# A hybrid pooling and attention layer: the gates by tanh in place of exponential, addition, reciprocal and product

## The reference, cut to what matters

```python
hn = _rmsnorm(h, norm_g[layer])
proj = hn @ w_in[layer]
pv, pg, q, k, v, ag = jnp.split(proj, SPLITS, axis=-1)
pool_out = _multiscale_pool(pv, pool_w[layer], pool_scale[layer])
attn_out = _attention_branch(q, k, v, q_norm_g[layer], k_norm_g[layer], sinks[layer])
mixed = jnp.concatenate([jax.nn.silu(pg) * pool_out,
                         jax.nn.silu(ag) * attn_out], axis=-1)
h = h + mixed @ w_out[layer]
```

## Time and profile before

| what | value |
|---|---|
| three runs | 1301.02, 1302.70 and 1302.71 us, median 1302.7 us |
| span of the profiled execution | 1300.8 us |
| the profiled execution's own time | not given apart from its span |
| TensorE busy (matmul) | 1279.3 us, 98% of the span |
| VectorE busy | 895.0 us, 69% |
| ScalarE busy | 634.8 us, 49% |
| TensorE clock granted | full (1.000 on average) |
| HBM traffic | 103 GB/s on average |

### The profile page before, as it was taken

One profiled execution on the slowest core, in us unless ns is written; L12 is line 12 of the kernel. 1 busy time (PEld: TensorE's weight loads), 2 busy tenths in 40 slices (PEclk: granted clock), 3 DMA queues, 4 the chain that ended last, 5 costly groups with the idle time before them and its releaser, 6 DMA issues.

```text
span 1300.8 us, 19299 instructions
## 1 busy us (share of the span) xinstructions
PE 1279.3 (98%) x6200; PEld 1057.4 (81%) x6200; DVE 895.0 (69%) x1417; ACT 634.8 (49%) x1490; POOL 66.5 (5%) x78
## 2 busy tenths in 40 slices
PE   4999999999999999999999999999999999999998
PEld 4988798798888987888888887787887877788887
DVE  7466777878868777665644677777787887854553
ACT  6434356365454554545433344554645545444442
POOL 0000000010010110000000000000101103000000
PEclk9999999999999999999999999999999999999999
DMA  5233322322322225544543332223222222244442
GB/s 213 79 92 97 90 72 75 89 68 63 94 81 75 67 73 185 188 133 157 186 127 89 92 98 86 70 73 88 83 72 79 84 81 74 93 141 137 161 140 86
DMA packets 70609, 134.38 MB, mean 103 GB/s; under 512 B 8064, under 2 KB 10240, under 8 KB 69888
## 3 DMA queue, kind: packets, MB, share of 16 engines
q1 hardware_dynamic: 68160, 125.17, 31.4%
q0 software_dynamic: 2384, 8.39, 1.8%
HBM read 125.14 MB, written 8.39 MB: 103 GB/s over the span
## 4 chain that ended last, share of the span: by engine, by line
PE 94%; DVE 3%; DMA 1%; ACT 1%; issue 1%; SPq 0%; ACTq 0%
PE R L1058 18%; PE R L1059 18%; PE R L1062 18%; PE S L1281 4%; PE S L1282 4%; PE S L1280 4%; PE S L1181 3%; PE S L1180 3%; PE OP L1282 2%; PE OP L1280 2%; PE R L1281 2%; PE OP L1281 2%; PE R L1282 2%; PE R L1280 2%; PE OP L1059 1%; PE OP L1062 1%
## 5 line engine op out<-in xcount | busy, mean ns | idle before, releaser
L430 ACT ACTIVATE wh<-raw 128x512 fp32r<-128x512 f32 x400 | 250.3, 631 | 534.7 <-PE R L1062 310.1
L725 DVE TENSOR_TENSOR wl<-raw,wh 128x512 fp32r<-128x512 f32 x400 | 281.7, 708 | 264.7 <-ACT wh L430 263.6
L1058 PE MATMUL R<-act_h,wh 128*128 128x512 f32 (+1 forms) x1168 | 426.0, 370 | 0.0
L1059 PE MATMUL R<-act_l,wh 128*128 128x512 f32 (+1 forms) x1168 | 422.8, 367 | 0.0
L1062 PE MATMUL R<-act_h,wl 128*128 128x512 f32 (+1 forms) x1168 | 403.5, 366 | 0.0
L1058 PEld LDWEIGHTS R<-act_h,wh 128*128 128x128 f32 x1168 | 220.1, 188 | 36.4 <-DVE wl L725 0.8
L1059 PEld LDWEIGHTS R<-act_l,wh 128*128 128x128 f32 x1168 | 220.1, 188 | 34.7
L1062 PEld LDWEIGHTS R<-act_h,wl 128*128 128x128 f32 x1168 | 210.6, 188 | 36.7
L948 DVE RECIPROCAL scr<-scr 128x512 f32<-128x512 f32 x32 | 107.3, 3353 | 1.1
L402 POOL TENSOR_TENSOR scr<-scr 128x527 f32<-128x527 f32 (+3 forms) x40 | 48.7, 1217 | 837.6 <-ACT pv_last L430 378.2
L430 ACT ACTIVATE pm<-OP 16x128 fp32r<-16x128 f32 x256 | 68.1, 266 | 5.4
(11 more groups left out here) (210 smaller groups left out, 1844.5 us busy)
## 6 DMA issues: line engine op xcount, KB each, us to landing
raw<-w_in_blocks SPq DMA_DIRECT2D x272, 256.0 KB, 2.6
raw<-w_out_in SPq DMA_DIRECT2D x128, 256.0 KB, 3.0
scr<-xcat SPq DMA_DIRECT2D x32, 256.0 KB, 4.4
mixed<-xcat SPq DMA_DIRECT2D x4, 1024.0 KB, 7.7
res<-xcat SPq DMA_DIRECT2D x16, 256.0 KB, 3.2
out<-scr POOLq DMA_DIRECT2D x14, 256.0 KB, 2.6
out<-res POOLq DMA_DIRECT2D x14, 256.0 KB, 4.2
scr<-pool_w_in SPq DMA_DIRECT2D x8, 256.0 KB, 3.0
```

The costliest lines, as they stand in the source:

```text
L430: return nc.scalar.activation(dst, src, ACT.Copy)
L725: return nc.vector.tensor_tensor(dst, a, b, ALU.subtract)
L1058: mm(o, wh[:, b, w], act_h[:, k, c], start=(k == 0), stop=False)
L1059: mm(o, wh[:, b, w], act_l[:, k, c], start=False, stop=False)
```

## The change

The gate tile u is read from PSUM as before. ScalarE now writes tanh(u/2) in place of exp(-u). VectorE forms (tanh(u/2) + 1) times u in one instruction with two operations, in place of three instructions. This is twice the gate, so each use is halved: `o_out` multiplies by 0.5 in the same instruction as the gate, and `mix_out` takes the per-channel scale from a small table `hscale` of halved scales, which is written once at the start. Two semaphores are no longer needed. Waits, slots and the order of everything else stay.

```diff
+        hscale = sb("hscale", [P, PAIRS])
...
-        s_ga = sem("s_ga")
-        s_gr = sem("s_gr")
...
-                        nc.scalar.activation(gate[n], bank[:, :], ACT.Exp, scale=-1.0).then_inc(s_ge[n], 1)
+                        nc.scalar.activation(gate[n], bank[:, :], ACT.Tanh, scale=0.5).then_inc(s_ge[n], 1)
...
+            nc.vector.tensor_scalar(hscale[:, :], vec[:, V_SCALE:V_SCALE + PAIRS], 0.5, None, ALU.mult).then_inc(s_gq, 1)
             nc.vector.tensor_scalar(gq8[:, :], vec[:, V_GQ:V_GQ + 1], HD ** -0.5, None, ALU.mult).then_inc(s_gq, 1)
-            dve.wait_ge(s_gq, 1)
+            dve.wait_ge(s_gq, 2)
...
-                        vec[:, bass.ds(V_SCALE + g * 2 + jj, 1)], gate[2 + jj].unsqueeze(1),
+                        hscale[:, bass.ds(g * 2 + jj, 1)], gate[2 + jj].unsqueeze(1),
                         ALU.mult, ALU.mult).then_inc(s_me, 1)
...
-                        nc.vector.tensor_tensor(mixed[:, bass.ds(PAIRS + g * 2 + u // 2, 1), cols],
-                                                o_sum.unsqueeze(1), gate[u // 2][:, cols].unsqueeze(1),
-                                                ALU.mult).then_inc(s_oe, 1)
+                        nc.vector.scalar_tensor_tensor(mixed[:, bass.ds(PAIRS + g * 2 + u // 2, 1), cols],
+                                                       o_sum.unsqueeze(1), 0.5, gate[u // 2][:, cols].unsqueeze(1),
+                                                       ALU.mult, ALU.mult).then_inc(s_oe, 1)
...
-                        nc.vector.tensor_scalar(gate[n], gate[n], 1.0, None, ALU.add).then_inc(s_ga, 1)
-                        dve.wait_ge(s_ga, G * 4 + n + 1)
-                        nc.vector.reciprocal(gate[n], gate[n]).then_inc(s_gr, 1)
-                        dve.wait_ge(s_gr, G * 4 + n + 1)
-                        nc.vector.tensor_tensor(gate[n], bank[:, :], gate[n], ALU.mult).then_inc(s_gt[n], 1)
+                        nc.vector.scalar_tensor_tensor(gate[n], gate[n], 1.0, bank[:, :],
+                                                       ALU.add, ALU.mult).then_inc(s_gt[n], 1)
```

## The result

The changed kernel takes 1304.4 us, the kernel before 1302.5 us beside it (medians of 20 runs each). One of the changed kernel's 20 runs took 2101.7 us at a granted TensorE clock of 0.558 and is left out of the ratio; it doesn't move the median. The ratio is 1.0015, with a 95% interval of 1.0009 to 1.0022. So it is slower by 1.9 us (1.2 to 2.9). It stays within the 0.2% that the prediction called no change, but it goes the other way than forecast and lies outside the range of 1298.3 to 1303.3 us. The profiled run took 1304.25 us, with a span of 1302.6 us: 1.65 us lie outside the span.

A forecast was written before the change was run, and what follows sets the result against it. TensorE was taken as the bound, with VectorE's savings hidden except at waits for lines 940 and 739: -1.22 - 0.74 + 0.0 = -1.96, say -2.0 us, from 1302.7 to 1300.7 us; range 1298.3 to 1303.3 us.

The forecast's parts named there:

- `hscale` is one tiny instruction at the start: Writing the halved scales at the start: hidden, at most 0.1 us if the semaphore is slow.
- New waits.* None.: Across the kernel: no new waits, since banks are free earlier but TensorE waited for none; no transfer added.
- a change in the products' pace: Sign of a wrong prediction: TensorE's products starting closer together once VectorE is quieter; no size given.
- another cause: Slower by over 0.2% for a reason not named; chance 1%.
- (a): Output projection's fourth bank, waiting for the last `o_out` (line 940): wait gone in both halves, 2 x 0.61 = 1.22 us gained.
- (b): Wait for line 739, whose frames load after both `mix_out` of group 3: loads some 7 us earlier, 0.74 us gained.
- The three steps that the prediction priced: TensorE's lost time at two waits for line 940 and one for line 739: 0.61 + 0.61 + 0.74 = 1.96 us.
- both bounds (691 and 742): New VectorE gate instruction, in ns: 691 is the plain product from PSUM, 742 is line 871's two-operation form, the value taken.
- rival C: ScalarE: tanh and exp need different tables, 51 us of loads; 1301.5 us if hidden (5%), over 2.6 us slower (5%).
- Rival A: End of group 3: VectorE's time counts, two reciprocals worth 7.4 us in the first half, 1295.3 us; chance 6%.
- B: Only the edges: the frames' chain is held by something else, the 0.74 us stay, 1301.5 us; chance 15%.
- D: The change does nothing: the edge waits have another cause just as late, for instance `o_part`, 1302.7 us; chance 2%.

The follow-up runs named there:

- pad alone: The kernel before, with an unused tensor of 32 bytes per partition where the change puts `hscale`, instructions unchanged: 1306.1 us, ratio 1.003.
- hscale last: The changed kernel with `hscale` allocated behind the last tensor, so every other tensor stands where it stood before the change: 1299.6 us, ratio 0.998.
- the kernels with 128 and 256 unused bytes: The changed kernel with `hscale` behind the last tensor and 128 or 256 unused bytes ahead of `junk`: 1305.2 us and 1300.0 us.
- the four kernels with the gain and the old distances: Changed kernel, `hscale` last: 1299.6 us; also 256 bytes ahead of `junk`: 1300.0; or 64 ahead of all tensors: 1299.8; kernel before, 4 gates changed: 1299.9.
- the run with 4 short gates: The kernel before with the new form only for the third and fourth gate of group 3 in each half, halved scales last: 1299.9 us, ratio 0.9978.

## Why the prediction was wrong

**The step that failed** is the one on new tensors: "`hscale` is one tiny instruction at the start", 0 to 0.1 us, and with it "*New waits.* None." as the end of the list of costs. It costed what the new tensor does in instructions, and not what it does to the placement of others, which it put at nothing without a reason. The missing term is + 3.5 us measured alone (1306.1 against 1302.6, interval 2.3 to 5.6) and + 4.8 us with the change in place (1304.4 against 1299.6). The traces put 0.6 us of the difference between the two on the waits, which the slower products shorten while they are there; the rest is inside the scatter. The prediction did name a change in the products' pace among the things that would make it wrong, but tied it to VectorE's load, for which there was nothing, and gave it no chance. No rival had this mechanism; "another cause" got 1%.

Where the time went can be told by the numbers of the products, which are the same 6200 in the same order in all traces. Time from one product to another, us:

| products | stage | before | after | pad alone | hscale last |
|---|---|---|---|---|---|
| 0 to 48 | start | 13.09 | 12.36 | 12.05 | 12.26 |
| 48 to 2500 | first half, up to group 3 | 442.50 | 442.12 | 442.12 | 442.48 |
| 2500 to 3000 | its end, projection begins | 110.80 | 110.43 | 111.50 | 109.26 |
| 3000 to 3500 | projection, then keys and values | 111.19 | 112.40 | 112.39 | 111.20 |
| 3500 to 5400 | second half, up to group 3 | 424.35 | 424.29 | 424.29 | 424.36 |
| 5400 to 5500 | its end | 23.17 | 22.63 | 23.26 | 22.38 |
| 5500 to 6199 | projection | 160.15 | 162.72 | 162.72 | 160.15 |

The pace costs 1.2 and 2.6 us in the projection's two plain stages. The 0.4 us that the move gains in the first half's groups is not explained.

**(a) and (b), the waits.** Right in place and in size. With the placement held, the two ends of group 3 gained 1.54 and 0.79 us, 2.33 in all, against 1.35 and 0.61, 1.96 in all. The three steps that the prediction priced give back 0.61, 0.61 and 0.73 us, 1.95 in all. Two things it didn't price make up nearly all of the rest. The step behind each wait is longer than its neighbours as well (the next product started at 489.01 after 488.70, so 0.31 us and not 0.23): 0.08, 0.08 and 0.05 us. And there was a small wait that the view of waits doesn't list: in each half one product in the fourth weight block, at 494.98 in the first, takes 0.29 us to the next instead of 0.23; with the change it is gone, 0.06 us each. The prediction's "nothing else in the middle of the kernel is lost to a wait" is wrong by that much. The 104 us in other groups gained nothing, as said.

**The rest of the 3.0 us.** These two traces also differ by 0.83 us at the start. It isn't the change: the kernels with 128 and 256 unused bytes, which have the new gates, start as late as before (13.12 and 13.09 us to product 48), and the old gates with the pad as early as 12.05. The trace of before shows when the pace rises: products of 264 columns are 0.22 us apart until 22.86, and 0.12 us apart from 24.22 on.

```profile
22.42 0.42 PE L1058 MATMUL R<-act_h,wh 128*128 128x264 f32 x1
22.64 0.42 PE L1059 MATMUL R<-act_l,wh 128*128 128x264 f32 x1
...
24.22 0.28 PE L1059 MATMUL R<-act_l,wh 128*128 128x264 f32 x1
24.34 0.28 PE L1058 MATMUL R<-act_h,wh 128*128 128x264 f32 x1
```

The granted clock in the rows is 1.00 on either side of it, so they don't say what raises the pace. In the 14 traces of this study product 48 starts anywhere from 23.96 to 24.99 us, with no order by kernel. That is 1 us of the 2 to 3 us by which runs of one kernel differ. One pair of traces can't explain a difference of medians; but the four kernels with the gain and the old distances lie 3.0, 2.5, 2.7 and 2.6 us under before, and 2.33 us is inside each interval.

**Durations.** 684 ns for the new instruction, under both bounds (691 and 742): with an immediate scalar it costs no more than the plain product. 473 and 459 ns for the two forms of the halved `o_out`, where the plain products took 478 and 465: the guess was 0.03 us more, and it costs nothing. 589 ns for tanh, exactly that of the exponential. Six table loads, as before, four of them at the copy's line: rival C did not take place. VectorE's busy time came out at 780, 2 us above the span I gave.

**Rival A** (VectorE's time counts, 1295 us) is refuted by the runs: both gates at each end are short in the run with 4 short gates, which is 2.6 us faster than before and not 7.4. **B** (the frames' wait stays): with the change the row is gone. **D** likewise.

**The profiled time.** The span was held against the runs of other executions. The profiled run of the changed kernel shows 1.65 us between span and time. So the profile of before stood for about 1302.5 us, the median, and not for the fastest run. It changed nothing in the sum, which was a difference. The low end of the range was put at 1298.3 us where its own sum gives 1298.5; that changes nothing either.

## What to carry to other kernels

A change that allocates, drops or resizes a tensor is two changes: diff the addresses of all tensors before and after, and put the new one last, or pad to the old layout, before you price or measure the rest. When an engine is busy for its whole span, count instructions in a fixed stretch, as its pace can change without any wait. If matrix operands stream from SBUF back to back, try the starts of the stationary and the moving operand at equal residues modulo 256 bytes; starting a tile some columns later in its tensor can be enough (1302.6 to 1299.6 us here, without one instruction changed).

## What the runs showed of the hardware

- Products of 128 x 128 by 512 columns in fp32r followed one another in 227.1 to 227.3 ns when the stationary and the moving operand started at equal residues modulo 256 bytes, and in 232.7 to 232.8 ns when all eight operand tiles, or seven of them, were off by something between 32 and 224 bytes (only multiples of 32 were tried, and the residues rest on the layout assumed above); that is 2.4% of the pace. With three of eight off it was 229.4 ns. A shift of both by 64 bytes changed nothing. In the groups such distances gave 231.2 ns (all at 0, with the other changes of that run), 231.9 (one in four) and 232.9 (none). Which part of reading or loading the operands collides is not shown; the load of the next stationary tile runs beside the current product, so a conflict of the two reads is a guess. Why the groups don't reach 227 ns wasn't settled.
- The Trainium skill, "SBUF — State Buffer", section "Operand start alignment", asks only that an operand start at a multiple of its element size, and says of its own measurements that they are about legality and not speed. All the starts here obey that; the runs show a difference in speed among them.
- A VectorE instruction with two operations, an immediate scalar and one PSUM operand took 684 ns at 128 x 512, one with a scalar from SBUF 740 to 750 ns (line 871, before and after).
- Tanh of a tile of 128 x 512 from PSUM took ScalarE 589 ns, as the exponential did, and with both in the kernel there were six table loads, as with the exponential alone.
